# Head pairs of an attention layer on half arrays: both heads in turn, row halves for scores, column halves for values

## The chip, the cores and the metric

One core of a Trainium2 chip runs the whole program in one launch. The metric is the device time of an execution in microseconds; the median of three runs before the change is 1536.01 us.

## The reference, cut to what matters

Two request groups (a prompt of 512 tokens and a sample of 64 tokens with a cache of 512) go through a trunk of two layers. Layer 0 mixes tokens with "fox" attention, softmax attention with a forget gate; layer 1 with "stick", stick-breaking attention. Both have 12 heads of width 64, and in both 4 more heads read 256 memory tokens. All is float32.

```python
def fox_block(q, k, v, cq, ck, qpos, kpos):
    s = einsum('bqhd,bkhd->bhqk', q, k) * SCALE
    s = s + cq[..., :, None] - ck[..., None, :]
    p = softmax(where(kpos <= qpos, s, -inf)); return einsum('bhqk,bkhd->bqhd', p, v)
def sb_block(q, k, v, qpos, kpos):
    z = einsum('bqhd,bkhd->bhqk', q, k) * SCALE
    u = where(kpos < qpos, log_sigmoid(-z), 0)
    rest = cumsum(u, axis=3, reverse=True) - u
    a = where(kpos < qpos, exp(log_sigmoid(z) + rest), 0); return einsum('bhqk,bkhd->bqhd', a, v)
# each layer: proj = rmsnorm(x) @ w_in -> q, k, v, q_mem; o = [mixer heads, memory heads]
#   x = x + o @ w_out;  x = x + (silu(gate) * up) @ w_down, with rmsnorm(x) @ w_gate_up = gate, up
```

## The kernel before, in words

Activations lie feature-major: 128 features on the partitions, 576 tokens (64 sample, 512 prompt) along the row. Every projection is a row of slabs of 128 output columns; the weight and the activation are each split in a high and a low part, and `passes` (L556) issues three products for each of the eight row blocks, over two halves of 288 tokens: six passes, called a piece. ACT makes the high part of a slab (L840), POOL the low part (L473).

Attention runs in calls, one for a pair of heads: two memory calls (`mem0`, `mem1`), then six pair calls, in each layer. A call has nine units (UNITS = 2 x QT + 1): for each head four blocks of 128 prompt queries (units 0 to 3 and 4 to 7), and unit 8, the sample's queries of both heads. Block i of a pair has (i + 1) x 128 keys, unit 8 has 576; all units of a memory call have 256. On its way a unit goes from PE (`scores`, L607) to DVE (`front`, L1146; in stick ACT's `softplus`, L911, comes first), to ACT (exponential), in fox and memory calls to DVE again (normalize), to PE (`turn`, L645, transposes into `turned`) and to ACT (copy to `pt`). `values` (L657) multiplies `pt` with the values of four blocks, `values_sample` (L672) does it for unit 8, and `out_high` and `out_low` split the result on ACT and DVE into `o_hi` and `o_lo`.

Which half of the array belongs to which head is hidden by zeros: `queries` (L1137) writes a head's 64 query rows in a tile `qz` whose other 64 rows POOL has zeroed (`zero_rows`, L485), so a score product runs over all 128 rows. A value product has both heads' 128 columns, of which half are used.

The order of the work is written out by hand in each engine's `attention` (PE L686, ACT L965, DVE L1234). At step u (0 to 8) PE does `spread[u]` pieces of the next call's projections with the leftovers of the previous call between them (step 0: its unit 8 transposed and its second head's values; step 1: its sample), then transposes unit u - 1, then issues the scores of unit u + 2. A steady pair call spreads 24 pieces as (2, 2, 4, 3, 3, 2, 3, 3, 2). The first head's values come at step 5. There are two score buffers; PE's wait on `score_free` for unit u counts that unit u - 2 has gone through `front`. At step u ACT does softplus(u + 1) in stick, the exponential of u, the copy of u - 1 and, where a projection tile starts, `high`. DVE does front(u + 1), normalizes u, and takes finished tiles out. The last call of a layer has the output projection beside it, with few pieces.

SP issues all loads in order; the caches of a call wait until the call two before it is done.

Of the kernel before, what the change touches and what calls it, by code (L numbers as in the profile page):

```python
# [35 lines left out]
P = 128  # L36
D_MODEL = 1024
SEQ = 512
# [54 lines left out]
def build(nc, x_t, mem_t, w_mkv, w_in, w_f, w_out, w_gu, w_dn, gains, b_f, ck, cv, clf, cmk, cmv,  # L93
# [4 lines left out]
    def sb(name, shape, dt=F32, stack=ctx):  # L98
# [29 lines left out]
    qz = [at(f"qz{i}", [P, 2, TOK]) for i in range(2)]  # L128
# [8 lines left out]
    pt = at("pt", [P, QT, SEQ])  # L137
# [4 lines left out]
    ckbs = [at(f"ckbs{i}", [P, KEYS_S]) for i in range(2)]  # L142
    cum = at("cum", [HEADS, PAST + TOK])
# [21 lines left out]
    spare = [tile[:, 0:SLAB] for tile in (qz[0][:, :, :].rearrange("p h c -> p (h c)"),  # L165
                                          qz[1][:, :, :].rearrange("p h c -> p (h c)"), kb[0], kb[1],
                                          vcs[:, :, :, :].rearrange("p i j c -> p (i j c)"),
                                          vs[:, :, :, :].rearrange("p i j c -> p (i j c)"))]
    mvt = pt[:, :, 0:N_MEM]
    m_sum = sumsq[:, 0:N_MEM]  # L170
    m_sq = pt[:, :, :].rearrange("p j (a c) -> p (j a) c", a=2)
# [101 lines left out]
    class Call:  # L273
# [5 lines left out]
        def __init__(self, layer, half, par, mem=False, tiles=(), spread=(0,) * UNITS, fill=0):  # L279
# [11 lines left out]
            self.out = (a + layer * ATTNS) * 3  # L291
# [34 lines left out]
        def width(self, u):  # L326

            if u == 2 * QT:
                return N_MEM if self.mem else KEYS_S
            return N_MEM if self.mem else (u % QT + 1) * P  # L330
# [33 lines left out]
    def _(sp):  # L364
# [10 lines left out]
        def cache(layer, half, par, mem):  # L375

            c = Call(layer, half, par, mem)
            at_least(sp, out_ready, 0 if layer == 0 and mem else c.out - 3)
# [9 lines left out]
            if layer == 0:  # L388
# [3 lines left out]
                sp.wait_ge(cum_out, 16)  # L392
                for hd in range(2):
# [74 lines left out]
    def _(pool):  # L468
# [16 lines left out]
        def zero_rows(layer):  # L485
# [3 lines left out]
            for par in range(2):  # L489
                tiles += [qz[par][HD:P, 0, :], qz[par][0:HD, 1, :], qs[par][HD:P, 0:DEC], qs[par][0:HD, DEC:]]  # L490
# [57 lines left out]
    def _(pe):  # L548
# [58 lines left out]
        def scores(c, u):  # L607

            if u == 0:
                pe.wait_ge(qkv_ready, c.qk)  # L610
            sample = u == 2 * QT
            hd, i = divmod(u, QT)
            if sample:
                pe.wait_ge(cache_in[c.par], c.caches)
                query = qs[c.par][:, :]
                if not c.mem:
                    pe.wait_ge(out_free, c.out + 1)
                keys, own = kb[c.par], 0
            else:
                query = qz[c.par][:, hd, DEC + i * P:DEC + (i + 1) * P]  # L620
                keys, own = (mk[:, c.layer, c.par, :], 0) if c.mem else (kb[c.par], KEYS_S)
            pe.wait_ge(score_free, c.use + (u - 1))
            parts = c.parts(u)
            for n, (out, cols) in enumerate(parts):
                masked = c.stick and n == len(parts) - 1
                mm = pe.matmul(out, query, keys[:, own + cols.start:own + cols.stop],  # L626
                               start=True, stop=not masked)
            if c.stick:

                mask = mask_b[:, P:] if sample else mask_b[:, 0:P]  # L630
                out, width = parts[-1][0], mask.shape[-1]
                mm = pe.matmul(out[:, out.shape[-1] - width:], ident_b[:, :], mask, start=False, stop=True)
# [53 lines left out]
        def attention(c, prev, nxt):  # L686
# [22 lines left out]
            if prev is None:  # L709
                scores(c, 0)  # L710
                scores(c, 1)
            for u in range(UNITS):
# [12 lines left out]
                if u == QT + 1:  # L725
                    values(c, 0)
# [716 lines left out]
```

## Time and profile before

| | |
|---|---|
| median of 3 runs | 1536.01 us (1534.1 to 1536.88) |
| span of the profiled execution | 1535.0 us |
| TensorE (PE) busy | 1471.1 us, 96% |
| VectorE (DVE) busy | 656.7 us, 43% |
| ScalarE (ACT) busy | 576.1 us, 38% |
| GpSimd (POOL) busy | 525.5 us, 34% |
| mean granted TensorE clock | 0.996 |

The profiled execution is known by its span, from the first to the last instruction; its own time is not given apart from it, and the median of the runs is 1.0 us above the span. PE's busy time is modelled: a pass is shown longer than the distance between two starts.

### The profile page before, as it was taken

Reading aid. Unit: us, or ns where it says so; the run is one execution under the profiler, and the core shown is the slowest. Engines: PE = TensorE matmul, PEld = TensorE weight load, DVE = VectorE, ACT = ScalarE, POOL = GpSimd, SP = SyncE. Lnnn points to the kernel's source line nnn. Section 1 sums busy time; section 2 is a strip of 40 time slices with the busy share of each in tenths; the row PEclk is TensorE's granted clock in tenths of the full one; section 3 lists DMA queues with packets and bytes.
Section 4 is the critical chain, followed back from the end, with each engine's and each line's share of the span. In section 5 each row is a group of like instructions: output and inputs, shape, how many; then the busy total and the mean of one; then the engine's idle time right before and its main releaser. Section 6 shows DMA issues by size and latency. Waiting matters only on the chain.

```text
span 1535.0 us, 27449 instructions
## 1 busy us (share of the span) xinstructions
PE 1471.1 (96%) x10463; PEld 1394.0 (91%) x10463; DVE 656.7 (43%) x1035; ACT 576.1 (38%) x1054; POOL 525.5 (34%) x251
## 2 busy tenths in 40 slices
PE   5899999899999999999999999988999999999996
PEld 5788888699999999999987888868999999999996
DVE  6678777722333333311237666664233333330002
ACT  5454444433222222222235766774422222222211
POOL 1512112134444444344441111112544444443442
PEclk9999999999999999999999999999999999999998
DMA  6223432112222222222231222211222222222231
GB/s 251 72 63 100 130 125 92 56 56 91 81 82 81 81 81 82 86 77 86 78 94 38 89 88 82 71 57 41 83 83 82 82 82 82 82 79 82 83 89 72
DMA packets 42877, 130.25 MB, mean 85 GB/s; under 512 B 5148, under 2 KB 7196, under 8 KB 42688
## 3 DMA queue, kind: packets, MB, share of 16 engines
q1 hardware_dynamic: 38160, 121.23, 26.0%
q10 hardware_dynamic: 4656, 8.21, 1.4%
q8 instruction: 38, 0.62, 0.2%
q14 instruction: 23, 0.19, 0.0%
HBM read 118.85 MB, written 10.57 MB: 84 GB/s over the span
## 4 chain that ended last, share of the span: by engine, by line
PE 83%; DVE 7%; ACT 4%; issue 2%; DMA 1%; DVEq 1%; ACTq 1%; SPq 0%; POOL 0%; POOLq 0%
PE acc L556 72%; PE out_ps L668 4%; PE score L626 3%; PE turned L640 2%; DVE work_c L1160 2%; DMA w_raw<-in_w_in 1%; ACT w_hi L840 1%; PE out_ps L679 1%; DVE work_a L1164 1%; DVE work_a L1157 1%; DVE qz L1133 1%; DVE least L1191 1%; ACT work_c L921 1%; ACT work_c L919 1%; DVE work_b L1198 1%
## 5 line engine op out<-in xcount | busy, mean ns | idle before, releaser
L473 POOL TENSOR_TENSOR w_lo<-w_raw,w_hi 128x1024 fp32r<-128x1024 f32 (+1 forms) x190 | 462.5, 2434 | 856.4 <-ACT w_hi L840 855.9
L556 PE MATMUL acc<-xg_hi,w_hi 128*128 128x288 f32 x2048 | 463.2, 308 | 0.8 <-POOL w_lo L473 0.8
L840 ACT ACTIVATE w_hi<-w_raw 128x1024 fp32r<-128x1024 f32 (+1 forms) x194 | 202.2, 1042 | 640.5 <-PE acc L556 626.4
L556 PE MATMUL acc<-xg_hi,w_lo 128*128 128x288 f32 x2048 | 438.6, 296 | 0.0
L556 PE MATMUL acc<-xg_lo,w_hi 128*128 128x288 f32 x2048 | 437.9, 295 | 0.0
L556 PEld LDWEIGHTS acc<-xg_hi,w_hi 128*128 128x128 f32 x2048 | 332.3, 189 | 20.8 <-issue 13.4
L556 PEld LDWEIGHTS acc<-xg_hi,w_lo 128*128 128x128 f32 x2048 | 329.6, 189 | 0.0
L556 PEld LDWEIGHTS acc<-xg_lo,w_hi 128*128 128x128 f32 x2048 | 329.1, 188 | 0.0
L556 PE MATMUL acc<-f_hi,w_hi 128*128 128x288 f32 x704 | 151.1, 296 | 0.0
L556 PE MATMUL acc<-f_lo,w_hi 128*128 128x288 f32 x704 | 149.8, 293 | 0.0
L556 PE MATMUL acc<-f_hi,w_lo 128*128 128x288 f32 x704 | 148.9, 293 | 0.0
L1295 DVE TENSOR_TENSOR x<-acc,x 128x576 f32<-128x576 f32 x32 | 24.2, 757 | 284.5 <-PE acc L556 284.5
L1131 DVE TENSOR_TENSOR work_c<-acc,rstd 128x576 f32<-128x576 f32 x44 | 33.4, 758 | 244.3 <-PE acc L556 244.3
L556 PEld LDWEIGHTS acc<-f_lo,w_hi 128*128 128x128 f32 x704 | 112.8, 188 | 0.0
L556 PEld LDWEIGHTS acc<-f_hi,w_lo 128*128 128x128 f32 x704 | 112.4, 187 | 0.0
L556 PEld LDWEIGHTS acc<-f_hi,w_hi 128*128 128x128 f32 x704 | 111.9, 187 | 0.0
L1320 DVE TENSOR_TENSOR f_lo<-work_c,f_hi 128x576 f32 x44 | 84.3, 1915 | 42.2 <-ACT f_hi L1047 42.2
L935 ACT ACTIVATE pt<-turned 128x256 f32<-128x256 f32 (+3 forms) x128 | 53.7, 419 | 108.7 <-PE turned L640 108.5
L482 POOL TENSOR_TENSOR sumsq<-sumsq,work_c 128x576 f32<-128x576 f32 x34 | 50.0, 1469 | 123.2 <-ACT work_c L861 123.1
L640 PE MATMUL turned<-cst,work_b 128*128 128x128 f32 x372 | 68.2, 279 | 15.3 <-DVE work_b L1198 10.4
L626 PE MATMUL score<-kb,qz 128*128 128x128 f32 (+1 forms) x192 | 69.2, 442 | 9.8 <-DVEq L1166 9.8
L1131 DVE TENSOR_TENSOR work_a<-acc,rstd 128x576 f32<-128x576 f32 x44 | 33.4, 758 | 90.1 <-PE acc L556 76.4
(148 smaller groups left out, 1620.1 us busy)
## 6 DMA issues: line engine op xcount, KB each, us to landing
w_raw<-in_w_gu SPq DMA_DIRECT2D x88, 512.0 KB, 3.6
w_raw<-in_w_in SPq DMA_DIRECT2D x40, 512.0 KB, 6.0
w_raw<-in_w_dn SPq DMA_DIRECT2D x32, 512.0 KB, 3.5
w_raw<-in_w_out SPq DMA_DIRECT2D x16, 512.0 KB, 3.6
w_raw<-in_w_dn SPq DMA_DIRECT2D x16, 384.0 KB, 3.1
out_k_o<-kb ACTq DMA_DIRECT2D x12, 288.0 KB, 5.1
out_v_o<-vf_z ACTq DMA_DIRECT2D x12, 288.0 KB, 6.9
kb<-in_ck SPq DMA_DIRECT2D x12, 256.0 KB, 2.6
```

The costliest lines, as they stand in the source:

```text
L473: pool.tensor_tensor(w_lo[par][:, 0:cols], raw(s, par, cols), w_hi[par][:, 0:cols].bitcast(F32), ALU.subtract).then_inc(wlo_made, 1)
L482: pool.tensor_tensor(sumsq[:, :], sumsq[:, :], work_c[:, m % 2, :], ALU.add) \
L556: mm = pe.matmul(acc[:, tpar, h, 0:c1 - c0], w[par][:, k * P:(k + 1) * P], a[:, c0:c1], start=first and n == 0, stop=last and n == 2)
L626: mm = pe.matmul(out, query, keys[:, own + cols.start:own + cols.stop], start=True, stop=not masked)
L640: mm = pe.transpose(turned[:, j * P:(j + 1) * P], tile[:, j * P:(j + 1) * P], ident)
L668: mm = pe.matmul(out_ps[:, c0:SEQ], val, pt[:, j, c0:SEQ], start=(j == 0), stop=(j == count - 1), skip_group_check=True)
L840: act.activation(w_hi[par][:, 0:cols], raw(s, par, cols), ACT.Copy).then_inc(whi_made, 1)
L935: act.activation(out, src, ACT.Copy).then_inc(turned_free, 1)
L1131: last = dve.tensor_tensor(halves(out), src, halves(rstd[rows, :]), ALU.mult)
L1160: dve.tensor_tensor_scan(tail[:, ::-1], wide[:, ::-1], wide[:, ::-1], 0.0, ALU.add, ALU.bypass)
L1295: dve.tensor_tensor(halves(x[:, m, :]), acc[:, m % 2, :, 0:HALF], halves(x[:, m, :]), ALU.add).then_inc(x_new, 1)
L1320: dve.tensor_tensor(f_lo[:, bass.ds(j, 1), :], work_c[:, 0:1, :], f_hi[:, bass.ds(j, 1), :].bitcast(F32), ALU.subtract).then_inc(flo_made, 1)
```

## The change

A head's queries are no longer padded: one tile `q` holds both heads. Both heads of a block of queries are units 2i and 2i + 1. `scores(c, i)` issues both, head 0 on rows 0 to 63 and head 1 on rows 64 to 127, at steps 0, 2 and 4 of the call (row 0 at step 7 of the call before), after waiting for both buffers; the sample's scores go at step 6. `values` runs once for both heads, at step 0 of the next call, with head 0 on output columns 0 to 63 and head 1 on 64 to 127, alternating over the key blocks; `pt` becomes two tiles. Outputs of a call are counted 2 instead of 3, and the prompt output is split by one operation each on ACT and DVE. To make room, `ckbs` and `cum` share memory, for which SP waits once more.

```diff
@@ -125,7 +125,8 @@
     at = lambda name, shape, dt=F32: sb(name, shape, dt, region)
-    qz = [at(f"qz{i}", [P, 2, TOK]) for i in range(2)]
+    qb = at("qb", [P, 2, TOK])
+    q = [qb[:, i, :] for i in range(2)]
     qs = [at(f"qs{i}", [P, 2 * DEC]) for i in range(2)]
     kb = [at(f"kb{i}", [P, PAST + TOK]) for i in range(2)]
     vcs = at("vcs", [P, 2, QT, P])
...
@@ -390,6 +392,7 @@
                 sp.wait_ge(cum_out, 16)
+                sp.wait_ge(turned_ready, 2 * DEPTH + 1)
...
@@ -604,32 +607,42 @@
             if s and (s - 1) % MKV_TILES >= 2:
                 turn_mem(s - 1)
-        def scores(c, u):
-
-            if u == 0:
+        def mask_on(c, u, out):
+
+            mask = mask_b[:, P:] if u == 2 * QT else mask_b[:, 0:P]
+            width = mask.shape[-1]
+            return pe.matmul(out[:, out.shape[-1] - width:], ident_b[:, :], mask, start=False, stop=True)
+
+        def scores(c, i):
+
+            if i == 0:
                 pe.wait_ge(qkv_ready, c.qk)
-            sample = u == 2 * QT
-            hd, i = divmod(u, QT)
-            if sample:
-                pe.wait_ge(cache_in[c.par], c.caches)
-                query = qs[c.par][:, :]
-                if not c.mem:
-                    pe.wait_ge(out_free, c.out + 1)
-                keys, own = kb[c.par], 0
-            else:
-                query = qz[c.par][:, hd, DEC + i * P:DEC + (i + 1) * P]
-                keys, own = (mk[:, c.layer, c.par, :], 0) if c.mem else (kb[c.par], KEYS_S)
-            pe.wait_ge(score_free, c.use + (u - 1))
-            parts = c.parts(u)
+            pe.wait_ge(score_free, c.use + 2 * i)
+            keys, own = (mk[:, c.layer, c.par, :], 0) if c.mem else (kb[c.par], KEYS_S)
+            cols = slice(DEC + i * P, DEC + (i + 1) * P)
+            outs = [score[:, c.buf(2 * i + hd), 0:c.width(2 * i)] for hd in range(2)]
+            for hd in range(2):
+                rows = slice(hd * HD, (hd + 1) * HD)
+                mm = pe.matmul(outs[hd], q[c.par][rows, cols], keys[rows, own:own + c.width(2 * i)],
+                               start=True, stop=not c.stick)
+                if not c.stick:
+                    mm.then_inc(score_ready, 1)
+            if c.stick:
+                for hd in range(2):
+                    mask_on(c, 2 * i + hd, outs[hd]).then_inc(score_ready, 1)
+
+        def scores_sample(c):
+
+            pe.wait_ge(cache_in[c.par], c.caches)
+            if not c.mem:
+                pe.wait_ge(out_free, c.out)
+            pe.wait_ge(score_free, c.use + (2 * QT - 1))
+            parts = c.parts(2 * QT)
             for n, (out, cols) in enumerate(parts):
-                masked = c.stick and n == len(parts) - 1
-                mm = pe.matmul(out, query, keys[:, own + cols.start:own + cols.stop],
-                               start=True, stop=not masked)
+                mm = pe.matmul(out, qs[c.par][:, :], kb[c.par][:, cols],
+                               start=True, stop=not c.stick or n < len(parts) - 1)
             if c.stick:
-
-                mask = mask_b[:, P:] if sample else mask_b[:, 0:P]
-                out, width = parts[-1][0], mask.shape[-1]
-                mm = pe.matmul(out[:, out.shape[-1] - width:], ident_b[:, :], mask, start=False, stop=True)
+                mm = mask_on(c, 2 * QT, parts[-1][0])
             mm.then_inc(score_ready, 1)
         def turn_blocks(n, tile, blocks, beside=None):
...
@@ -654,26 +667,27 @@
                 turn_blocks(c.turned_round(2 * QT) + 1,
                             work_b[:, c.buf(2 * QT), KEYS_S - P:KEYS_S], 1)
-        def values(c, hd):
-
-
-            pe.wait_ge(turned_free, c.turned_round(QT * (hd + 1) - 1) + 1)
-            if hd and not c.mem:
+        def values(c):
+
+            pe.wait_ge(turned_free, c.turned_round(2 * QT - 1) + 1)
+            if not c.mem:
                 pe.wait_ge(score_free, c.used(2 * QT))
-            at_least(pe, out_free, c.out + hd)
+            at_least(pe, out_free, c.out)
             count = MB if c.mem else QT
             for j in range(count):
                 c0 = 0 if c.mem else j * P
-                val = mv[:, c.layer, c.par, j * P:(j + 1) * P] if c.mem else v[c.par][:, j, :]
-                mm = pe.matmul(out_ps[:, c0:SEQ], val, pt[:, j, c0:SEQ], start=(j == 0),
-                               stop=(j == count - 1), skip_group_check=True)
+                for hd in range(2):
+                    rows, cols = slice(hd * HD, (hd + 1) * HD), slice(j * P + hd * HD, j * P + (hd + 1) * HD)
+                    val = mv[:, c.layer, c.par, cols] if c.mem else v[c.par][:, j, rows]
+                    mm = pe.matmul(out_ps[rows, c0:SEQ], val, pt[hd][:, j, c0:SEQ], start=(j == 0),
+                                   stop=(j == count - 1), skip_group_check=True)
             mm.then_inc(out_ready, 1)
         def values_sample(c):
             pe.wait_ge(turned_free, c.turned_round(2 * QT) + (1 if c.mem else 2))
             if not c.last:
-                pe.wait_ge(out_free, c.out + 2)
+                pe.wait_ge(out_free, c.out + 1)
             count = MB if c.mem else QT
             for j in range(count):
                 mm = pe.matmul(c.sample_out(), vc[c.par][:, j, :], pts[:, j * P:(j + 1) * P],
...
@@ -708,41 +722,40 @@
             if prev is None:
                 scores(c, 0)
-                scores(c, 1)
             for u in range(UNITS):
                 pieces = c.spread[u]
                 half = pieces // 2
                 fill(pieces - half)
                 if u == 0 and prev is not None:
                     turn(prev, 2 * QT)
-                    values(prev, 1)
+                    values(prev)
                     turn_rest(prev)
                 if u == 1 and not c.mem:
                     pe.wait_ge(qkv_ready, c.qkv)
                     turn_blocks(c.round, vf[:, DEC:], QT)
                 if u == 1 and prev is not None:
                     values_sample(prev)
-                if u == QT + 1:
-                    values(c, 0)
                 fill(half)
                 if u:
                     turn(c, u - 1)
-                if u + 2 < UNITS:
-                    scores(c, u + 2)
-                elif nxt is not None:
-                    scores(nxt, u + 2 - UNITS)
+                if u in (0, 2, 4):
+                    scores(c, u // 2 + 1)
+                elif u == 6:
+                    scores_sample(c)
+                elif u == 7 and nxt is not None:
+                    scores(nxt, 0)
             if nxt is None:
                 fill(2)
                 turn(c, 2 * QT)
                 fill(1)
-                values(c, 1)
+                values(c)
                 turn_rest(c)
                 fill(1)
                 values_sample(c)
                 fill(1)
-                pe.wait_ge(out_free, c.out + 3)
+                pe.wait_ge(out_free, c.out + 2)
                 for n in range(2):
                     passes(n, PAIRS - 1, o_hi[:, PAIRS - 1, :], o_lo[:, PAIRS - 1, :], n, False, True) \
                         .then_inc(slab_done, 1)
...
@@ -938,11 +951,11 @@
             n = c.width(u) // P
             if u < 2 * QT:
-                i = u % QT
+                i, hd = divmod(u, 2)
                 if u == 0 and not c.mem:
                     act.wait_ge(turned_ready, c.turned_round(u) + 1)
                     act.activation(vn[c.par][:, :], turned[:, P:2 * P], ACT.Copy)
-                copy_round(c.turned_round(u), pt[:, 0:n, i * P:(i + 1) * P],
+                copy_round(c.turned_round(u), pt[hd][:, 0:n, i * P:(i + 1) * P],
                            turned[:, 0:n * P].rearrange("p (j q) -> p j q", j=n))
                 return
             copy_round(c.turned_round(u), pts[:, 0:n * P], turned[:, 0:n * P])
...
@@ -953,13 +966,14 @@
             act.wait_ge(out_ready, c.out + (n + 1))
             tile = bass.ds(c.o_tile, 1)
+            if n == 0:
+                act.activation(o_hi[:, tile, DEC:], out_ps[:, :].rearrange("p (a c) -> p a c", a=1),
+                               ACT.Copy).then_inc(out_hi, 1)
+                return
             for hd in range(2):
-                if n != 1 - hd:
-                    rows = slice(hd * HD, (hd + 1) * HD)
-                    cols = slice(0, DEC) if n == 2 else slice(DEC, TOK)
-                    src = c.sample_out()[rows, hd * DEC:(hd + 1) * DEC] if n == 2 else out_ps[rows, :]
-                    last = act.activation(o_hi[rows, tile, cols],
-                                          src.rearrange("p (a c) -> p a c", a=1), ACT.Copy)
+                rows = slice(hd * HD, (hd + 1) * HD)
+                src = c.sample_out()[rows, hd * DEC:(hd + 1) * DEC]
+                last = act.activation(o_hi[rows, tile, 0:DEC], src.rearrange("p (a c) -> p a c", a=1), ACT.Copy)
             last.then_inc(out_hi, 1)
         def attention(c, prev, nxt):
...
@@ -1140,13 +1152,12 @@
-            return tile_out(slab, tpar, [(qz[par][0:HD, 0, :], slice(0, HD), scale),
-                                         (qz[par][HD:P, 1, :], slice(HD, P), scale)])
+            return tile_out(slab, tpar, [(q[par], slice(0, P), scale)])
```

## Rows read from the trace of the kernel before

**Rows 1.** The page: busy time of the engines; TensorE's granted clock in 40 slices
```profile
PE 1471.1 (96%) x10463; PEld 1394.0 (91%) x10463; DVE 656.7 (43%) x1035; ACT 576.1 (38%) x1054; POOL 525.5 (34%) x251
PEclk9999999999999999999999999999999999999998
```

**Rows 2.** Windows, one fox and one stick call: busy of PE, PEld, DVE, ACT, POOL
```profile
140.90:174.30 33.40, 33.40 (x222) 29.47 (x221) 25.98 (x57) 14.82 (x37) 7.10 (x4) 1.00 0.33 106
902.60:939.20 36.60, 34.72 (x231) 29.90 (x230) 24.38 (x40) 25.28 (x57) 7.14 (x4) 1.00 0.24 75
```

**Rows 3.** PE's waits, 110 to 276 and 833 to 1060 us: total, times, longest
```profile
PE out_ps L668 <- ACT pt L935: 0.6, 1, 0.6
...
PE score L626 <- DVEq L1166: 9.8, 10, 1.6
```

**Rows 4.** Groups of instructions by line, whole span
```profile
L626 PE MATMUL score<-kb,qz 128*128 128x128 f32 (+1 forms) x192 | 69.2, 442 | 9.8 <-DVEq L1166 9.8
L668 PE MATMUL out_ps<-pt,vs 128*128 128x512 f32 (+1 forms) x192 | 56.2, 436 | 0.9 <-ACT pt L935 0.8
...
L626 PE MATMUL score<-mk,qz 128*128 128x256 f32 x64 | 19.1, 385 | 1.3 <-DVEq L1189 1.3
...
L668 PE MATMUL out_ps<-pt,mv 128*128 128x512 f32 x32 | 15.1, 593 | 0.0
```

**Rows 5.** Chain of waits in a fox call: start us, us, work
```profile
141.08 0.22 PE score L626 x2
...
143.42 0.43 PE score L626 x2
...
145.21 2.16 PE out_ps L668 x8
...
152.27 0.86 PE score L626 x2
153.13 3.18 PE acc L556 x24
```

**Rows 6.** PE timeline, from 12-column passes to full ones: start us, us
```profile
61.73 0.29 PE L768 MATMUL score<-xg_hi,wf_lo 128*12 128x288 f32 x1
61.87 0.42 PE L556 MATMUL acc<-xg_hi,w_hi 128*128 128x288 f32 x2
```

**Rows 7.** Chain of waits in a stick call, steps 6 and 7
```profile
935.34 0.23 PE turned L640 x2
...
935.87 1.05 ACT w_hi L840
...
938.35 0.69 ACT work_c L921
...
939.96 1.36 DVE work_c L1160
```

**Rows 8.** PE timeline of the same steps, idle time in brackets
```profile
939.24 0.39 PE L626 MATMUL score<-kb,qz 128*128 128x128 f32 x2
...
942.32 0.70 PE L626 MATMUL score<-kb,qz 128*128 128x256 f32 x2 [0.57 <-DVEq L1166]
```

**Rows 9.** Groups by shape, 850 to 1050 us, width 384: busy, mean ns
```profile
L919 ACT ACTIVATE work_c<-work_c 128x384 f32<-128x384 f32 x11 | 5.8, 524 | 0.7
...
L1160 DVE TENSOR_TENSOR_SCAN work_c<-work_a 128x384 f32<-128x384 f32 x11 | 10.5, 958 | 0.8
...
L1157 DVE SCALAR_TENSOR_TENSOR work_a<-score,work_c 128x384 f32<-128x384 f32 x11 | 6.1, 558 | 13.5 <-ACT work_c L921 13.5
```

**Rows 10.** Chain of waits in a stick call, step 1 to 2
```profile
914.89 0.12 PE turned L642
...
916.81 0.60 ACT work_c L916
```

**Rows 11.** Timeline of a fox call, step 7, DVE and PE
```profile
173.32 1.41 DVE L1188 TENSOR_TENSOR work_a<-work_a,cst 128x64 f32<-128x64 f32 x1
...
174.34 0.39 PE L626 MATMUL score<-kb,qz 128*128 128x128 f32 x2
```

More of the change, by code:

```diff
@@ L136, in build @@
     vf = vf_z[:, DEC:]
-    pt = at("pt", [P, QT, SEQ])
+    pt = [at(f"pt{i}", [P, QT, SEQ]) for i in range(2)]
     pts = at("pts", [P, QT * P + P])
@@ L141, in build @@
     ckb = [gates[:, i] for i in range(2)]
-    ckbs = [at(f"ckbs{i}", [P, KEYS_S]) for i in range(2)]
-    cum = at("cum", [HEADS, PAST + TOK])
+    ckbs_cum = at("ckbs_cum", [P, 2 * KEYS_S])
+    ckbs = [ckbs_cum[:, i * KEYS_S:(i + 1) * KEYS_S] for i in range(2)]
+    cum = ckbs_cum[0:HEADS, 0:PAST + TOK]
     wf_raw = at("wf_raw", [P, KT * HEADS])
@@ L162, in build @@
     f_lo = sb("f_lo", [P, FT, TOK], F32R)
[L165 to L166 removed]
+    spare = [tile[:, 0:SLAB] for tile in (qb[:, :, :].rearrange("p i c -> p (i c)"),
+                                          pt[1][:, :, :].rearrange("p j c -> p (j c)"), kb[0], kb[1],
                                           vcs[:, :, :, :].rearrange("p i j c -> p (i j c)"),
                                           vs[:, :, :, :].rearrange("p i j c -> p (i j c)"))]
[L169 removed]
+    mvt = pt[0][:, :, 0:N_MEM]
     m_sum = sumsq[:, 0:N_MEM]
[L171 removed]
+    m_sq = pt[0][:, :, :].rearrange("p j (a c) -> p (j a) c", a=2)
     psum = lambda name, shape: ctx.enter_context(nc.psum_tensor(name, shape, F32))
@@ L290, in __init__ @@
                 a * PAIR_ROUNDS + (start + MEM_PAIRS * (MEM_ROUNDS - PAIR_ROUNDS))
-            self.out = (a + layer * ATTNS) * 3
+            self.out = (a + layer * ATTNS) * 2
             self.qkv = layer * IN_TILES + a + 1 if mem else a * 3 + (layer * IN_TILES - 1)
@@ L329, in width @@
                 return N_MEM if self.mem else KEYS_S
-            return N_MEM if self.mem else (u % QT + 1) * P
+            return N_MEM if self.mem else (u // 2 + 1) * P
         def turned_round(self, u):
@@ L377, in cache @@
             c = Call(layer, half, par, mem)
-            at_least(sp, out_ready, 0 if layer == 0 and mem else c.out - 3)
+            at_least(sp, out_ready, 0 if layer == 0 and mem else c.out - 2)
             if mem:
@@ L489, in zero_rows @@
             for par in range(2):
-                tiles += [qz[par][HD:P, 0, :], qz[par][0:HD, 1, :], qs[par][HD:P, 0:DEC], qs[par][0:HD, DEC:]]
+                tiles += [qs[par][HD:P, 0:DEC], qs[par][0:HD, DEC:]]
             for n, tile in enumerate(tiles):
@@ L781, in _ @@
                              ident[0:HEADS, 0:HEADS]).then_inc(turned_ready, 1)
-            pe.wait_ge(zeroed, 9 * (layer + 1))
+            pe.wait_ge(zeroed, 5 * (layer + 1))
             pe.wait_ge(masks_made, 1)
@@ L975, in attention @@
                     copy_turned(prev, 2 * QT)
-                    out_high(prev, 1)
+                    out_high(prev, 0)
                 if u == 1 and not c.mem:
@@ L981, in attention @@
                 if u == 1 and prev is not None:
-                    out_high(prev, 2)
-                if u == QT + 1:
-                    out_high(c, 0)
+                    out_high(prev, 1)
                 if u in c.starts:
@@ L999, in attention @@
                 copy_turned(c, 2 * QT)
+                out_high(c, 0)
                 out_high(c, 1)
-                out_high(c, 2)
         for layer in range(DEPTH):
@@ L1204, in out_low @@
             tile = bass.ds(c.o_tile, 1)
+            if n == 0:
+                dve.tensor_tensor(o_lo[:, tile, DEC:], out_ps[:, :].rearrange("p (a c) -> p a c", a=1),
+                                  o_hi[:, tile, DEC:].bitcast(F32), ALU.subtract).then_inc(out_free, 1)
+                return
             for hd in range(2):
-                if n != 1 - hd:
-                    rows = slice(hd * HD, (hd + 1) * HD)
-                    cols = slice(0, DEC) if n == 2 else slice(DEC, TOK)
-                    src = c.sample_out()[rows, hd * DEC:(hd + 1) * DEC] if n == 2 else out_ps[rows, :]
-                    last = dve.tensor_tensor(o_lo[rows, tile, cols],
-                                             src.rearrange("p (a c) -> p a c", a=1),
-                                             o_hi[rows, tile, cols].bitcast(F32), ALU.subtract)
+                rows = slice(hd * HD, (hd + 1) * HD)
+                src = c.sample_out()[rows, hd * DEC:(hd + 1) * DEC]
+                last = dve.tensor_tensor(o_lo[rows, tile, 0:DEC], src.rearrange("p (a c) -> p a c", a=1),
+                                         o_hi[rows, tile, 0:DEC].bitcast(F32), ALU.subtract)
             last.then_inc(out_free, 1)
@@ L1248, in attention @@
                 if u < 2 and prev is not None:
-                    out_low(prev, u + 1)
-                if u == QT + 1:
-                    out_low(c, 0)
+                    out_low(prev, u)
                 if u in c.ends and c.tiles[0][1] != "o":
@@ L1254, in attention @@
             if nxt is None:
+                out_low(c, 0)
                 out_low(c, 1)
-                out_low(c, 2)
         for layer in range(DEPTH):
```

2 lines of the change are left out of this document (1 added, 1 removed).

## The prediction

> **What bounds the kernel now.** I read the page first. PE is busy for 96% of the span at a granted clock of nine tenths or more nearly throughout, which is its level of 2.4 GHz; DVE and ACT are far below it [rows 1]. So a microsecond less on PE counts wherever PE doesn't wait for somebody. The change touches only the two attention stages, about 250 us each. The windows over one steady call of each kind come next: a forgetting-attention pair takes 33.4 us and PE is busy in all of them; a stick-breaking pair takes 36.6 us with PE busy for 34.7 [rows 2]. The waits say the same: in the fox pairs PE waits 0.6 us in all, in the stick pairs 9.8 us, ten times, for the score buffer that DVE gives back [rows 3]. Fox is bound by PE's work; stick is bound by PE's work with the chain ACT, DVE, PE close behind. That second fact decides this forecast.
>
> **What the array halves can save.** Every f32 product stands in the trace as two records, two passes over its columns: the 96 score products of the pairs are 192 records, their 96 value products 192, the memory calls' 32 and 16 are 64 and 32 [rows 4]. A score product costs 0.86 us at 512 columns and 0.22 at 128, so 2.16 for the four widths of a head; a head's value products cost 2.16 too; six passes of the projection ("a piece") 3.18/4 = 0.80 [rows 5]; two transposes 0.23 [rows 7]. A pair call thus spends 4.3 us on scores and 4.3 on values. A memory call has eight score products of 256 columns (8 x 0.43 = 3.4) and four value products of 512 (4 x 0.86 = 3.4).
>
> No row shows a product on half the array beside another. A product on fewer columns of the array alone is not faster: the 128x12 passes start 0.13 us apart, as the full ones do [rows 6], so the whole gain is in overlap. Lower bound: none, 0 us. Upper bound: two heads for the price of one, half of 12 x 8.6 + 4 x 6.9 = 131, so 65 us. I take a case between. The instructions stay in the order a first pass, a second pass, b first pass, b second pass, and both passes of a head want the same half. If passes start in order, a's second runs with b's first, and b's second runs alone unless a new product of head a follows. Scores stand as lone pairs, so three passes remain of four: 4.3/4 = 1.1 us saved in a pair call, 0.85 in a memory call. Value products alternate over the key blocks, so they chain: the two heads cost 2.16 plus one last or first pass of 0.43, against 4.3; 1.7 saved, and in a memory call 3.4 - (1.7 + 0.43) = 1.3. Sum: 12 x 2.8 + 4 x 2.15 = **42 us saved on PE**.
>
> The Trainium skill, "TensorEngine Tiling (Array Packing)", Key Properties, says that tiles work in parallel, and that changing the tiling mode drains the engine. By the first half of that the upper bound would be possible. Before the change the nearest row to a change of mode, from a 128x12 pass to a full one, shows 0.14 us from start to start against 0.13 [rows 6]: no drain to be seen, and I charge none in the sum.
>
> **What the new order adds.** Before, the scores of unit u+2 are issued at the end of step u and need only unit u's front to be over. Now both heads' scores of a row of blocks are issued at the end of steps 0, 2 and 4 and need fronts u and u+1; the next call's first row is issued at step 7 and needs front 8. In each of these places PE asks for one front more, one step (2 to 4 pieces) earlier. Queued behind the waiting score on PE is all of the next step's projection, which nobody else can start.
>
> Step 7, stick. The chain of waits shows today's path: after the transposes at 935.3 come w_hi on ACT (1.05), the softplus activations of the 576-wide unit (0.69 each), then on DVE the maximum, the scan (1.36) and the subtraction [rows 7], and only then PE goes on at 942.32. The score product that will have to wait for it starts at 939.24 now [rows 8]. So PE will stand for 3.1 us there. Today the same chain ends 0.57 us late for a product one step further on.
>
> Step 4, stick, waiting for front 5 (384 wide): an activation is 0.52, a scan 0.96, the other DVE operations 0.56 [rows 9]. From the end of row 2's scores PE needs 3 pieces and two transposes, 2.6 us; then ACT copies (0.4), does w_hi (1.05) and softplus (3 x 0.52 and gaps, 1.7), DVE its 2.3: at 8.0 us the buffer is free. PE arrives at 2.6 + 3 x 0.80 + 0.2 = 5.2. Wait 2.8 us.
>
> Step 2, stick, front 3 (256 wide). ACT begins a softplus 1.9 us after the step's transposes end at 915.0, because copies and two DMA issues lie between [rows 10]; with 1.3 for softplus and 1.7 for DVE (the 384-wide ones less a quarter [rows 9]) the buffer is free at 5.0; PE needs 4 pieces and a transpose, 3.3. Wait 1.7 us. Step 6 waits for front 6 and comes out at 0.4; step 0 has the value products ahead of it and comes out at none.
>
> Sum for a stick call: 3.1 + 2.8 + 1.7 + 0.4 = 8.0 of waits, where 9.8/10 calls for two per call and so 1.9 today [rows 3]. **Added: 6.1 us a call, for six calls 37 us.** The last call has hardly any projection to lie beside, and I put it at the same.
>
> Fox fronts have no softplus on ACT, and their chain is shorter. The buffer of front 8 comes free after the mask addition that ends at 174.73; PE is there at 174.34 [rows 11]. So 0.4 to 0.5 there and, with a faster PE, about as much again for probabilities: 1.2 us a call, 7 in all. The memory calls get about 1 more in each layer, 2. In the last call of each layer, where PE waits for others at nearly each step, some 3 of the saved microseconds in all are not seen.
>
> Edits at no cost: one q tile written in place of two half ones (one operation less on DVE per call, beside PE); a single out_high and out_low for both heads; four memsets fewer per layer on POOL, beside the projection of the second tile. SP's new wait for the gate transposes stands behind its wait for cum's DMA, which starts later than they do, and the slab loads behind it aren't late. The value products moved from step 5 to step 0 of the next call wait for nothing new, as copies and the last front are done by then. Were that cover gone, each would cost at most its own few tenths in a call.
>
> **Sum.** 37 + 7 + 2 + 3 - 42 = +7 us on a span of 1535.0, which is 1542; the runs shown have their median 1.0 above this span, 1536.0, so **1543 us**.
>
> **Rivals.** (1) The halves overlap fully. Then 65 instead of 42 is saved; but with PE faster it meets more waits in fox (DVE is busy for 26.0 of 33.4 us [rows 2]), so about 15 more reach the end: 1528. This is the way to a faster kernel. For it: nothing forbids it but the order of passes. Against: order. (2) No overlap, or hardly any: f32 passes run one after the other. Then the 42 are gone, and with them the 3 that weren't seen and some 3 of waits: 1543 + 36 = 1579, since waits that start from PE's own issue stay as they are. For it: no row shows overlap. (3) Draining at each change between half and full array. A pass lasts 0.29 and one starts every 0.13 [rows 6], so a drain costs at most about the difference, 0.16; ten changes a call, 16 calls: 26 us, 1569. The page named above has that rule; against it stands the 0.14 of rows 6. (4) ACT and DVE lie far enough ahead that the waits are a third of what I walked, because the first of two fronts starts a step early: then 37 becomes some 15 and the time is 1521. Against: w_hi on ACT and its in-order queue are in the chain, whatever starts early.
>
> **How the numbers follow.** Main case 0.44; rival 1 0.12; rival 2 0.20; rival 3 0.14; rival 4 0.10. The main case's own range is 1533 to 1553. The measurement tells apart about 0.2%, 3 us. Rivals 1 and 4 are faster, less a part of 1 that falls within 3 us, and the low edge of the main case adds 0.02: faster 0.21. Within: 0.13. Slower: 0.66. The range from 1526 to 1582 leaves out rival 4, the upper part of rival 2 and the tails, about 2 in 10.
>
> **What would show it.** Score pairs with 64-row forms whose starts are less than a pass apart show overlap; their busy time should fall by a quarter, the value products' by 40%. The waits of PE for DVE's release of score should rise from 9.8 to some 40 us in layer 1, at steps 2, 4 and 7, and appear in fox at about 1 us a call. The stick call should lengthen from 36.6 to about 40 us, the fox call shrink from 33.4 to about 32. I am wrong if the stick call doesn't lengthen, or if PE's passes don't overlap at all.

## The result and the profile after

The changed kernel takes **1562.9 us** (median of 4, 1561.5 to 1563.6) against 1535.6 of the kernel before beside it: ratio 1.0176 with an interval of 1.0162 to 1.0191, 27 us slower. The forecast was slower by 7. The profiled execution's span went from 1535.0 to 1559.5.

The page: busy time of the engines, and TensorE's granted clock in 40 slices, as in [rows 1].

```profile
PE 1454.5 (93%) x10463; PEld 1364.9 (88%) x10463; DVE 629.4 (40%) x1003; ACT 566.3 (36%) x1038; POOL 523.0 (34%) x243
...
PEclk9999999999999999999999989988999999999998
```

PE is busy for 17 us less and the span is 25 longer, so waits came in. The clock row, even before, now has dips, in the slices of the stick stage. Its mean over the span is 0.975 of full speed, against 0.996 before.

Windows over a fox call and a stick call, columns as in [rows 2], where they took 33.40 and 36.60 us.

```profile
130.60:164.60 34.00, 31.37 (x222) 26.39 (x221) 25.08 (x54) 14.37 (x36) 7.12 (x3) 1.00 0.33 104
892.80:935.60 42.80, 35.49 (x231) 30.80 (x230) 22.61 (x39) 24.57 (x56) 7.99 (x3) 0.88 0.19 64
```

In the fox call PE works 2.0 us less and waits 2.6. The stick call is 6.2 us longer; PE is idle in 7.3 us of it, and is even busy for longer than before (35.5 against 34.7) at a mean clock of 0.88. Distances between the sample scores of neighbouring stick calls are 40.4 to 42.8 us, against 36.6 to 36.7 before; from the first to the last of that stage it is 262.1 against 230.0 us. The fox stage is 212.7 against 216.1.

Groups by line, whole span, which answer to [rows 4] (69.2, 56.2, 19.1 and 15.1 us there).

```profile
L626 PE MATMUL score<-kb,qb 64*128 64x128 f32 (+3 forms) x192 | 42.8, 525 | 46.5 <-DVEq L1177 42.8 <-DVEq L1200 3.5
L682 PE MATMUL out_ps<-pt,vs 128*64 128x512 f32 (+3 forms) x192 | 29.9, 455 | 0.0
L626 PE MATMUL score<-mk,qb 64*128 64x256 f32 x64 | 12.3, 463 | 1.9 <-DVEq L1200 1.9
L682 PE MATMUL out_ps<-pt,mv 128*64 128x512 f32 x32 | 7.7, 605 | 0.0
```

As many products as before, in 92.7 us instead of 159.6: 67 less. (Busy times are modelled and longer than the distance between starts, so the amount is rough; the starts below are exact.) The idle time ahead of the scores is the new item. PE's timeline, the places where a row of scores follows a step, idle time in brackets:

```profile
157.09 0.38 PE L653 MATMUL turned<-cst,work_b 128*128 128x128 f32 x2
157.40 1.13 PE L626 MATMUL score<-kb,qb 64*128 64x512 f32 x4
158.46 0.54 PE L559 MATMUL acc<-xg_hi,w_hi 128*128 128x288 f32 x2
158.83 0.43 PE L559 MATMUL acc<-xg_lo,w_hi 128*128 128x288 f32 x2
...
919.07 0.92 PE L626 MATMUL score<-kb,qb 64*128 64x384 f32 x4 [1.41 <-DVEq L1177]
928.22 1.13 PE L626 MATMUL score<-kb,qb 64*128 64x512 f32 x4 [2.75 <-DVEq L1177]
942.65 0.49 PE L626 MATMUL score<-kb,qb 64*128 64x128 f32 x4 [2.89 <-DVEq L1177]
```

Two 512-wide scores, four passes, take 1.06 us from their start to the next product's, where one takes 0.86 alone. In the records the first passes of the two heads start at 157.399 and 157.405, the second ones at 157.932 and 157.939. So the overlap is complete, and the order is first pass of both, then second pass of both; the 0.2 us above 0.86 is spent at the two ends of the block. Also to be seen: the first projection product after the block needs 0.37 to the next start, where the following need 0.27.

PE's waits, 60 to 330 us (fox) and, after the dots, 790 to 1100 us (stick): total, times, longest.

```profile
PE turned L653 <- DVE work_b L1209: 14.8, 15, 2.3
PE score L626 <- DVEq L1200: 4.2, 8, 0.7
...
PE score L626 <- DVEq L1177: 42.8, 17, 3.8
```

### The profile page after: what moved, and what is told of

Its sections match the earlier page's. It is cut to its first block, busy times and chain, and to the rows that moved or that the text cites. A ratio compares the mean times of both kernels' runs of the same rounds, so it can differ in the third digit from the quotient of the medians.

```text
span 1559.5 us, 27319 instructions
## 1 busy us (share of the span) xinstructions
PE 1454.5 (93%) x10463; PEld 1364.9 (88%) x10463; DVE 629.4 (40%) x1003; ACT 566.3 (36%) x1038; POOL 523.0 (34%) x243
## 4 chain that ended last, share of the span: by engine, by line
PE 77%; DVE 8%; ACT 5%; DVEq 3%; DMA 3%; issue 2%; ACTq 1%; SPq 1%; POOL 0%; POOLq 0%
PE acc L559 67%; PE score L626 2%; PE out_ps L682 2%; DMA w_raw<-in_w_in 2%; PE turned L653 2%; DVE work_c L1171 2%; DVEq L1195 1%; DVE work_b L1209 1%; ACT w_hi L853 1%; DVE work_a L1175 1%; DVE work_a L1168 1%; ACT work_c L932 1%; DVE least L1202 1%; ACT work_c L934 1%; PE out_ps L693 1%
## 5 line engine op out<-in xcount | busy, mean ns | idle before, releaser
L559 PE MATMUL acc<-xg_hi,w_hi 128*128 128x288 f32 x2048 | 457.6, 305 | 0.8 <-POOL w_lo L476 0.8
L559 PEld LDWEIGHTS acc<-xg_hi,w_lo 128*128 128x128 f32 x2048 | 333.6, 191 | 0.0
L559 PEld LDWEIGHTS acc<-xg_lo,w_hi 128*128 128x128 f32 x2048 | 333.6, 191 | 0.0
L653 PE MATMUL turned<-cst,work_b 128*128 128x128 f32 x372 | 73.0, 294 | 22.7 <-DVE work_b L1209 17.5
L626 PE MATMUL score<-kb,qb 64*128 64x128 f32 (+3 forms) x192 | 42.8, 525 | 46.5 <-DVEq L1177 42.8
L653 PEld LDWEIGHTS turned<-cst,work_b 128*128 128x128 f32 x372 | 48.8, 149 | 33.3 <-DVE work_b L1209 14.5
```

The lines of the kernel that those rows point to most:

```text
L559: mm = pe.matmul(acc[:, tpar, h, 0:c1 - c0], w[par][:, k * P:(k + 1) * P], a[:, c0:c1], start=first and n == 0, stop=last and n == 2)
L626: mm = pe.matmul(outs[hd], q[c.par][rows, cols], keys[rows, own:own + c.width(2 * i)], start=True, stop=not c.stick)
L653: mm = pe.transpose(turned[:, j * P:(j + 1) * P], tile[:, j * P:(j + 1) * P], ident)
```

## The experiments

Times of all are against the kernel before on the same chip, 1535.7 to 1536.9 us.

**half_alone**: the kernel before, in its own order, with half-array operands, so that no half product stands beside another of the other half.

```
-                query = qz[c.par][:, hd, ...]
+                query = qz[c.par][rows, hd, ...]
-                mm = pe.matmul(out_ps[:, c0:SEQ], val, pt[:, j, c0:SEQ], ...
+                mm = pe.matmul(out_ps[rows, c0:SEQ], v[..][:, j, rows], pt[:, j, c0:SEQ], ...
```

> The kernel before with its order of work, but every score product on 64 rows and every value product with 64 output columns, none beside another. If a product on half the array alone costs what a full one costs and the change of mode is free, the time is that of before, 1535 us. If each block costs about 0.4 us for going in and out, as the gaps around the blocks in the trace of the changed kernel suggest: 10 blocks a call, 4 us, over 16 calls 64 us, of which some is hidden in the last calls: 1580 to 1600 us.

Measured: 1574.8 us (1570.3 to 1581.4), ratio 1.0244 (1.0215 to 1.0273). Fox calls, 33.4 to 34.4 before, take 37.0, and PE is busy in all of it. Windows of a fox and a stick call, then the timeline of a score in the fox call:

```profile
151.15:188.11 36.96, 36.96 (x223) 28.71 (x222) 26.59 (x56) 14.93 (x37) 7.13 (x3) 1.00 0.29 96
900.60:938.10 37.50, 37.18 (x231) 28.86 (x230) 23.39 (x40) 25.52 (x56) 7.31 (x3) 1.00 0.23 73
```

```profile
141.63 0.60 PE L641 MATMUL turned<-cst,work_b 128*128 128x128 f32 x4
142.16 0.91 PE L627 MATMUL score<-kb,qz 64*128 64x384 f32 x2
143.00 0.53 PE L556 MATMUL acc<-xg_hi,w_hi 128*128 128x288 f32 x2
143.37 0.42 PE L556 MATMUL acc<-xg_lo,w_hi 128*128 128x288 f32 x2
```

A half-array product alone costs more than the full one. The last transpose to the score takes 0.20 us from start to start instead of 0.11, the score's first pass 0.43 instead of 0.32, its second pass 0.41 instead of 0.32, and the next full pass 0.24 instead of 0.13: together **0.40 us for going to half products and back**. This is the price that the forecast set at nothing. The Trainium skill, "TensorEngine Tiling (Array Packing)", Key Properties, has the rule that changing the tiling mode drains the engine; this trace agrees with it, by 0.40 us a block.

The kernel is 39 us slower than before, less than the 45 to 65 expected. Fox calls lose 3.1 us on average, near the 4 of ten blocks. Stick calls lose only 0.7 to 0.9 us, as PE's waits for scores there fall from 9.8 to 2.9 us: work that PE does instead of waiting costs nothing.

**head_outer**: the changed kernel with the two value loops exchanged, all key blocks of one head, then of the other.

```
-            for j in range(count):
-                for hd in range(2):
+            for hd in range(2):
+                for j in range(count):
```

> The changed kernel with the loops of the value products exchanged: all key blocks of head 0, then all of head 1. If passes of the two halves overlap only where the instructions alternate, a pair call's values go from 2.3 to about 4.3 us and the time rises by up to 16 x 1.9 = 30 us, less what waits hide, to 1575 to 1590. If the engine finds the other half's products anyway, the time stays at 1563.

Measured: 1583.4 us (1569.3 to 1590.8), ratio 1.0288 (1.0225 to 1.0351). The value products of a call, in the timeline of this kernel:

```profile
141.69 3.93 PE L682 MATMUL out_ps<-pt,vs 128*64 128x512 f32 x16
145.55 0.33 PE L653 MATMUL turned<-cst,work_b 128*128 128x128 f32 x1
```

and of the changed one:

```profile
140.28 2.37 PE L682 MATMUL out_ps<-pt,vs 128*64 128x512 f32 x16
142.59 0.33 PE L653 MATMUL turned<-cst,work_b 128*128 128x128 f32 x1
```

3.86 us against 2.31 from start to start, for the same sixteen passes. The 1.55 us, in 12 calls, are 19 us, and the medians differ by 20, though this kernel's runs scatter with its clock: mean 0.991 in the one of 1569.3 us, 0.969 in the one of 1590.8.

So the alternation is worth 1.55 us a pair call. But neighbours in the order aren't the only ones that overlap. Sixteen passes one after the other would be 4.3 us and the ends of the block, and 3.86 is less: in the records the first product of head 1 (512 columns) starts at 143.254, 6 ns behind the start of the third of head 0 (256 columns), which stands two products ahead of it, and before the fourth of head 0 has started. In the memory calls a head has only two value products, so the partner is always the one two places off, and there the exchange of the loops costs nothing. This kernel, then the changed one:

```profile
85.79 1.94 PE L682 MATMUL out_ps<-pt,mv 128*64 128x512 f32 x8
87.67 0.53 PE L559 MATMUL acc<-xg_hi,w_hi 128*128 128x288 f32 x2
```

```profile
86.31 1.94 PE L682 MATMUL out_ps<-pt,mv 128*64 128x512 f32 x8
88.17 0.53 PE L559 MATMUL acc<-xg_hi,w_hi 128*128 128x288 f32 x2
```

Both take 1.87 us from start to start. A product on the other half thus started beside one two places ahead of it; the partner four places ahead, which the pair calls would have needed, it didn't reach.

**pad_ahead and pad_paired**: the changed kernel's unit order (both heads of a row in turn) and its values side by side, but scores on the full array, against a query padded with zeros. In pad_ahead each score is issued by itself, two units ahead; in pad_paired both of a row are issued after one wait for both buffers, as in the change. To make room, one gate slab and the decay sums lie in tiles free at that time.

```
 pad_ahead, against the changed kernel
-            pe.wait_ge(score_free, c.use + 2 * i)
-                mm = pe.matmul(outs[hd], q[c.par][rows, cols], keys[rows, ...], ...
+            pe.wait_ge(score_free, c.use + (u - 1))
+            mm = pe.matmul(out, qz[c.par][:, hd, ...], keys[:, ...], ...
...
-                if u in (0, 2, 4):
-                    scores(c, u // 2 + 1)
+                if u + 2 < 2 * QT:
+                    scores(c, u + 2)
```

> The changed kernel with its value products as they are (side by side, both heads at step 0), but with the scores issued one unit at a time, two units ahead, over all 128 rows with zero-padded queries, as before the change; units still in the new order. Theory A (the loss is the paired wait for both score buffers, one front more and one step earlier): the stick call goes from 41.6 back to about 35 us, PE's waits for the score buffer in layer 1 from 42.8 to under 12 us, and the time is 1510 to 1522 us. Rival B (the loss is the new order of the units, which puts the wide ones side by side): the stick call stays above 39 us and the time above 1545. Rival C (the loss is changing between half and full array, seen as gaps of about 0.4 us a block): four of five blocks a call are gone, 16 x 4 x 0.4 = 26 us less, 1537, with the stick waits still there.

> As pad_ahead, but both heads' scores of a block row are issued together, after one wait for both buffers, at the steps of the changed kernel; over all 128 rows, so nothing of them overlaps and there is no change of array mode for scores. Theory A: the waits stay, the stick call stays at 41 to 43 us, the time 1555 to 1575. Rival C: 1540 or less. Against pad_ahead this run has only the paired wait more.

Measured: pad_ahead **1505.8 us** (1505.3 to 1508.3), ratio 0.9810 (0.9794 to 0.9826), faster than both kernels by 30 and 57, and 4 below the range of theory A. pad_paired 1576.7 (1576.2 to 1577.9), ratio 1.0268 (1.0251 to 1.0285), 2 above its range. Rivals B and C are out as the main cause. A fox and a stick call of pad_ahead, and its waits for scores at 780 to 1100 us:

```profile
131.40:164.50 33.10, 31.82 (x223) 27.82 (x222) 25.38 (x55) 14.27 (x36) 7.15 (x3) 1.00 0.32 108
843.40:876.60 33.20, 32.58 (x232) 28.28 (x231) 22.78 (x39) 24.66 (x56) 7.77 (x3) 1.00 0.25 83
```

```profile
PE score L623 <- DVEq L1176: 5.7, 8, 1.2
```

A stick call of pad_paired, and the same wait:

```profile
857.50:900.90 43.40, 36.06 (x229) 30.93 (x230) 22.87 (x39) 24.59 (x56) 7.94 (x3) 0.92 0.19 63
```

```profile
PE score L624 <- DVEq L1178: 44.2, 18, 3.8
```

The place and the form of the wait alone make 71 us, 10.2 in the stick call shown and 11 in those behind it: 5.7 us of waits in the stage become 44.2, the clock in the call falls to 0.92, and PE, with three passes fewer in its window, is busy for 3.5 us longer. Against this the half-array scores are worth little: the changed kernel is only 13.8 us faster than pad_paired. Complete overlap of the scores is 12 x 2.16 + 4 x 1.7 = 33 us, the changes of mode of 64 blocks are 26; what makes the remaining 7 of the 13.8 wasn't separated.

**old_order_values**: pad_ahead with its units head by head again as before; what is left of the change is the value products, moved to the end and side by side, and the single split of their output.

```
-            i, hd = divmod(u, 2)
+            hd, i = divmod(u, QT)
```

> pad_ahead with the units in the order of the kernel before (four blocks of head 0, then four of head 1): against the kernel before it has only the value products moved to the end and put side by side. Overlap alone should bring 12 x (4.3 - 2.3 - 0.4) + 4 x (3.4 - 1.7 - 0.4) = 24 us: 1512. If the new order of the units is itself worth something (pad_ahead has 1505.8, 30 us below before), this run is slower than pad_ahead, 1508 to 1516; if the order costs, it is faster, below 1503.

Measured: 1512.4 us (1510.5 to 1512.9), ratio 0.9848 (0.9831 to 0.9865), as expected. Values side by side are worth 23 us (overlap 12 x 2.16 + 4 x 1.7 = 33, less 16 blocks at 0.40 = 6, would be 26), and the unit order another 7. PE's waits for scores from 780 to 1100 us are 9.8 us here, as before the change, against the 5.7 of pad_ahead:

```profile
PE score L623 <- DVEq L1176: 9.8, 10, 1.6
```

**keep_busy**: the changed kernel with five products of a zero weight tile, two passes of 288 columns each, added to sums that stand open, ahead of the score waits of steps 4 and 7 in stick calls. PE's work grows; the data don't change.

```
+                if u in (4, 7) and c.stick and not c.last:
+                    for n in range(5):
+                        pe.matmul(acc[:, slot, 0, 0:HALF], zero_w[:, :], x[:, n, 0:HALF], start=False, stop=False)
```

> The changed kernel with five extra products (zero weights, f32, 288 columns, about 2.4 us together) in front of the score waits of steps 4 and 7 in the stick calls but the last; the sums stay as they are. The waits themselves can't get shorter. If the falling clock after a wait has its own share of the loss, the granted clock of a stick call goes from 0.88 back to near 1.00 and the time falls by 8 to 18 us, to 1545 to 1555. If the clock costs nothing, the time stays or rises by what the extra products exceed the waits, 1563 to 1568.

Measured: 1551.0 us (1550.3 to 1553.4), ratio 1.0096 (1.0077 to 1.0115): 12 us faster than the change, with a hundred passes more. A stick call:

```profile
894.70:934.10 39.40, 36.59 (x249) 30.41 (x249) 22.01 (x37) 24.34 (x56) 8.11 (x3) 1.00 0.21 70
```

The call's clock is 1.00 instead of 0.88, and the calls are 39.2 to 39.4 us instead of 40.4 to 42.8. What these products take away can be seen in the changed kernel behind the wait of 2.89 us at step 7, in its timeline:

```profile
942.65 0.49 PE L626 MATMUL score<-kb,qb 64*128 64x128 f32 x4 [2.89 <-DVEq L1177]
943.08 0.29 PE L614 MATMUL score<-mask_b,ident_b 128*128 128x128 bf16 x2
943.17 0.56 PE L559 MATMUL acc<-xg_hi,w_hi 128*128 128x288 f32 x2
943.53 0.69 PE L559 MATMUL acc<-xg_lo,w_hi 128*128 128x288 f32 x2
944.01 0.69 PE L559 MATMUL acc<-xg_hi,w_lo 128*128 128x288 f32 x2
...
946.64 0.64 PE L559 MATMUL acc<-xg_hi,w_hi 128*128 128x288 f32 x2
947.11 0.43 PE L559 MATMUL acc<-xg_lo,w_hi 128*128 128x288 f32 x2
```

From 943.53 on two passes take 0.48 us from start to start instead of 0.27. The granted clock from 943.5 to 946.9 us is 0.50: that is the clock's level of 1.2 GHz instead of 2.4, for some 3 us, after an idle stretch of 2.9 in busy work.

Not every such wait has this behind it. Of the ten waits of 2.75 us and more at steps 4 and 7 of these five calls, eight have; the first two, at 846.0 and 859.8 us, have not, and their products come every 0.27 us:

```profile
846.00 1.13 PE L626 MATMUL score<-kb,qb 64*128 64x512 f32 x4 [2.75 <-DVEq L1177]
...
847.51 0.43 PE L559 MATMUL acc<-xg_lo,w_hi 128*128 128x288 f32 x2
847.78 0.42 PE L559 MATMUL acc<-xg_hi,w_lo 128*128 128x288 f32 x2
```

And in a fox call of keep_busy itself, which took 38.5 us, the lower level came after waits of 0.80 and 0.62 us only (products 0.48 apart from 136.4 us on). What decides between the two levels isn't settled by these runs.

**late_high**: the changed kernel with the next weights' w_hi on ACT one step later, to take its 1.05 us out of the chain to step 4's scores. **pad_ahead_late** does the same to pad_ahead, **ahead_late_spread** also evens out how many pieces each step has, and **ahead_spread** does that alone.

```
+                late = 0 if c.mem or c.last else 1
-                if u in c.starts:
+                if u - late in c.starts:
...
-                        (2, 2, 4, 3, 3, 2, 3, 3, 2), fill)
+                        (2, 2, 3, 3, 3, 3, 3, 3, 2), fill)
```

> The changed kernel with ACT's w_hi in the pair calls (not the last) one step later, at steps 1, 4 and 7 in place of 0, 3 and 6. If w_hi (1.05 us) is in the chains that end PE's waits of 2.75 us at step 4 and 2.9 at step 7, these fall by about 1 us each in a stick call: 5 calls x 2 = 10 us less, and some more through the clock, 1545 to 1553 us. If the chain runs past it, the time stays at 1563.

> pad_ahead with w_hi one step later. PE waits only 0.6 to 0.8 us in a stick call and 0.6 to 1.5 in a fox call there, so at most 5 us are to be had: 1501 to 1506. With the scores two units ahead the same edit should bring far less than in the paired order.

> pad_ahead_late with the projection spread (2,2,3,3,3,3,3,3,2) in place of (2,2,4,3,3,2,3,3,2), for the order in which the wide units come late: one more piece lies before the step 6 wait for probabilities (1.5 and 0.6 us in the fox calls). 1497 to 1504 if that wait goes, no change if it only moves.

> pad_ahead with the projection spread (2,2,3,3,3,3,3,3,2) alone, w_hi where it was: the step 6 wait of the fox calls (0.6 to 1.5 us) is covered by one more piece. 1500 to 1505; no change if w_lo then comes late for the second tile, which the shift asks for at the same piece but sooner after w_hi.

Measured: late_high 1560.9 us (1560.6 to 1563.2), no difference to the change. Its score waits in the timeline:

```profile
923.80 0.92 PE L626 MATMUL score<-kb,qb 64*128 64x384 f32 x4 [2.21 <-DVEq L1178]
...
931.93 1.13 PE L626 MATMUL score<-kb,qb 64*128 64x512 f32 x4 [1.73 <-DVEq L1178]
...
945.62 0.49 PE L626 MATMUL score<-kb,qb 64*128 64x128 f32 x4 [3.26 <-DVEq L1178]
```

Step 4's wait fell by 1.0 us and step 2's grew by 0.8; step 7's is 3.26 in this call but 2.64 to 2.80 in the four others, against 2.89 to 3.20 in the change. In all, the waits for scores fell only from 42.8 to 40.9 us, and in fox a new one appeared, ahead of the projection (60 to 330 us):

```profile
PE acc L559 <- POOL w_lo L476: 9.7, 10, 1.5
```

In pad_ahead_late this new wait was 7.7 us in the same stretch and 4.0 in stick, and took the place of only 2.8 us of old ones (the wait for probabilities in fox, 11.7 to 8.9): 1517.6 us (1516.5 to 1518.7), 12 worse than pad_ahead. Spreading the pieces changed nothing with it (1517.6) or without it (1505.5, 1504.3 to 1508.2). The two with w_hi late came out worse than expected, and so did the spread on top: I had counted what left the score's chain and not that POOL's w_lo stands behind w_hi. The best version stays pad_ahead.

## Why the prediction was wrong in size

The direction held, and the wait for both buffers was a main cost as forecast; the sum did not hold. That the direction held is partly luck: with the overlap at its true size and all else as forecast, the sum would have been 7 - 23 = -16, faster; two costs that weren't in it turned it round. By terms, forecast and as the runs show them, in us:

| Term | forecast | shown |
|---|---|---|
| halves beside each other | -42 | -65 |
| changes between half and full array | 0 | +32 (80 blocks x 0.40) |
| score waits, stick | +37 | +33 (9.8 to 42.8) |
| waits, fox (60 to 330 us) | +7 | +11 (10.2 to 21.2) |
| clock | none | +12 at least |
| memory calls, last calls | +5 | not separated |
| sum | +7 | +23, against 24.5 in the span |

**Score waits in stick: right.** The chain was walked to 1.7, 2.8 and 3.1 us at steps 2, 4 and 7, and the trace has 1.41, 2.75 and 2.89 in the call shown above; the forecast "9.8 to some 40" came out at 42.8. The chain of waits ahead of step 7 is the one of [rows 7], one step early:

```profile
936.21 1.05 ACT w_hi L853
...
938.68 0.70 ACT work_c L934
...
940.29 1.36 DVE work_c L1171
...
941.73 0.69 DVE work_a L1175
```

That the term is this wait and no other is shown by pad_ahead, where the same work with the old look-ahead has 5.7 us of it.

**Overlap: the step that passes start in program order failed.** I let the second pass of head a run with the first of head b, and so kept three passes of four. The records show both first passes together and both second passes together, and head_outer shows a product that starts ahead of one that stands before it in the order. So the saving is all of my upper bound of 65 us; the busy time of the four groups fell by 67. The value block takes 2.31 us, most of its mode change included, not 2.16 + 0.43. So rival 1 had the overlap right; but it had no price for the changes of mode and the clock, and its 1528 is 35 too low.

**Changes of mode: the step "no drain to be seen" failed.** It rested on a 12-column pass next to a full one [rows 6], which costs nothing of the kind, while half_alone shows 0.40 us in and out for half products. I had counted ten changes at 0.16 at most as rival 3: 26 us against 32 shown. With 0.40 a block, lone rows of scores gain little: complete overlap saves 0.22 us at 128 columns and 0.86 at 512, 2.16 for four blocks, of which the changes take 1.6.

**Clock: the step was missing.** I read PE's clock row as flat [rows 1] and priced the waits at their own length. PE was then idle for nearly 3 us at a time in otherwise full work, and the products behind eight of ten such waits ran at the lower level. From 780 to 1100 us the mean granted clock is 0.91 in the change, 0.98 in keep_busy and 1.00 before. keep_busy gives at least 12 us back; it acts in five calls and at two waits of each, so this is a lower bound. PE's busy time allows an estimate too: it fell by 16.6 us in all, where -65 and +32 would make -33, which leaves 16 for products that ran slowly and for whatever else lengthened them. With the clock kept the stick call takes 39.3 us, about the 40 forecast. The two prices that I left out, mode and clock, make 44 us; that the overlap was 23 better than I took it hid half of them.

**Fox: "shrinks to about 32" failed.** The call stayed at 33.7 to 34.2. PE's 4.3 us of overlap went to five changes of mode (2.0) and to waits (2.6), above all the transposes' wait for DVE's normalized probabilities, 14.8 us against 7.4 before in the same window, 60 to 330 us:

```profile
PE turned L640 <- DVE work_b L1198: 7.4, 9, 2.2
```

That a faster PE meets DVE's chain in fox is what I had said of rival 1. The runs agree by steps: 10.8 us of this wait with only the value products overlapped (old_order_values), 11.7 with the new order too (pad_ahead), 14.8 with the half-array scores.

**Open.** The table's shown terms were each measured in another kernel or as a difference of waits; that they add up to the span within 2 us is partly luck, since the clock's term is a lower bound, the 0.40 comes from a block of scores, and a change of mode right behind a wait may cost less. The seven microseconds by which the half-array scores beat their account (pad_paired) belong here too.

## What to carry to other kernels

Put half-array products side by side, the two halves in turn, where they already stand together in long blocks and wait for nothing new, as the value products do here (23 us won); a lone pair must save more than 0.40 us to pay at all. Don't buy it with the look-ahead: a wait for both buffers cost 71 us, here more than the overlap could ever give. And price a long wait in a busy TensorE with the slow products that may stand behind it, not with its length alone; moving work out of one chain (w_hi) needs a look at who stands behind it (w_lo).

## What the runs showed of the hardware

- Two f32 products of 64 rows each, or of 64 columns each, run wholly beside each other when they are neighbours in the order, starts 6 to 7 ns apart. With 64 columns each they do so too when the partner is two places ahead (1.87 us a block in both orders, starts 13 to 14 ns apart); with the partner four places ahead most of the overlap is lost (3.86 us against 2.31), and a product of the second half starts ahead of one of the first that stands before it.
- Half-array products inside a stream of full ones cost 0.40 us per block, in and out; a 128x12 pass costs nothing of the kind.
- Of ten idle stretches of 2.75 to 3.2 us in full work, eight were followed by some 3 us or more at 1.2 GHz and two were not; zero products in them gave 12 us back.
